# Two products instead of three in every split fp32r projection of a two-block transformer kernel

## What is computed

```
mix = sigmoid(gate_a) * (y_a @ w_o_mla) + sigmoid(gate_b) * (y_b @ w_o_gla)
h = h + mix @ w_out
h = h + peer_ffn(rmsnorm(h, norm_ffn), peer_w_q, peer_keys, peer_u, peer_v)
```

## Time and profile before

| | us |
|---|---|
| median of three runs (lowest, highest) | 2176.15 (2173.21, 2176.32) |
| profiled execution, its span | 2175.9 |
| PE busy | 2115.4 (97%) |
| PE weight loads | 1661.6 (76%) |
| VectorE busy | 1304.1 (60%) |
| GpSimd busy | 1033.5 (47%) |
| ScalarE busy | 922.6 (42%) |
| a weight group's load, issue to landing (median) | 4.8 |

### The profile page before, as it was taken

How to read it: one execution, slowest core, us unless ns; L and a number is a source line. 1 busy time by engine, 2 the same in 40 slices (tenths; PEclk the granted TensorE clock), 3 DMA queues, 4 the chain that set the end, 5 groups by cost and what they waited for, 6 DMA issues and landing times.

```text
span 2175.9 us, 27394 instructions
## 1 busy us (share of the span) xinstructions
PE 2115.4 (97%) x10296; PEld 1661.6 (76%) x10296; DVE 1304.1 (60%) x2244; ACT 922.6 (42%) x1528; POOL 1033.5 (47%) x892
## 2 busy tenths in 40 slices
PE   8999999999999999999999998999999899999999
PEld 6877767557887776887878877777778788888887
DVE  6456257352235774215898957888881666666664
ACT  4223343572234234111334447777773434343432
POOL 6655546212324122877859887999996100000000
PEclk9999999999999999999999999999999999999999
DMA  5222312201111111233216664777788988888884
GB/s 201 100 78 78 116 61 90 90 30 49 59 40 59 59 55 43 97 122 110 78 59 199 205 206 141 272 289 246 272 291 294 333 300 286 289 284 300 288 287 149
DMA packets 98291, 359.32 MB, mean 165 GB/s; under 512 B 8480, under 2 KB 41504, under 8 KB 73328
## 3 DMA queue, kind: packets, MB, share of 16 engines
q1 hardware_dynamic: 98160, 357.56, 47.3%
HBM read 286.09 MB, written 71.30 MB: 164 GB/s over the span
## 4 chain that ended last, share of the span: by engine, by line
PE 67%; POOL 13%; DVE 11%; issue 6%; ACT 2%; DMA 1%; POOLq 0%; SPq 0%; ACTq 0%; DVEq 0%
PE ps L1438 11%; PE ps L1439 11%; PE ps L802 10%; PE ps L803 9%; PE ps L804 9%; POOL area L2643 6%; POOL wring_parts L2621 6%; PE ps L791 2%; PE ps L1249 2%; DVE area L2413 2%; PE ps L1386 1%; PE ps L1387 1%; DVE area L2410 1%; PE ps L884 1%; PE ps L1225 1%
## 5 line engine op out<-in xcount | busy, mean ns | idle before, releaser
L2577 POOL CAST wring_parts<-wring 128x512 fp32r<-128x512 f32 x236 | 170.5, 764 | 546.0 <-PE ps L804 429.3
L1386 PE MATMUL ps<-sqbuf_parts,wring_parts 128*128 128x512 f32 x1024 | 412.6, 403 | 5.5 <-POOL wring_parts L2621 5.5
L1387 PE MATMUL ps<-normed_x_parts,wring_parts 128*128 128x512 f32 x1024 | 404.4, 395 | 0.0
L2621 POOL TENSOR_TENSOR wring_parts<-wring_parts,wring 128x512 fp32r<-128x512 f32 x256 | 331.0, 1323 | 76.0 <-ACT wring_parts L1856 73.0
L2581 POOL TENSOR_TENSOR wring_parts<-wring,wring_parts 128x512 fp32r<-128x512 f32 x244 | 351.2, 1470 | 6.6 <-ACT wring_parts L1852 1.5
L1386 PEld LDWEIGHTS ps<-sqbuf_parts,wring_parts 128*128 128x128 f32 x1024 | 194.0, 189 | 50.6 <-POOL wring_parts L2621 4.9
L1387 PEld LDWEIGHTS ps<-normed_x_parts,wring_parts 128*128 128x128 f32 x1024 | 193.9, 189 | 41.8
L802 PE MATMUL ps<-resid_parts,wring_parts 128*128 128x512 f32 (+1 forms) x528 | 201.2, 381 | 6.1 <-DVE normed_x_parts L2010 3.3
L803 PE MATMUL ps<-normed_x_parts,wring_parts 128*128 128x512 f32 (+1 forms) x528 | 197.0, 373 | 0.0
L804 PE MATMUL ps<-resid_parts,wring_parts 128*128 128x512 f32 (+1 forms) x528 | 196.2, 372 | 0.0
L1474 ACT ACTIVATE area<-ps 128x1024 f32<-128x1024 f32 (+6 forms) x89 | 61.7, 696 | 275.2 <-PE ps L804 183.5
(11 more groups left out here) (269 smaller groups left out, 4431.4 us busy)
## 6 DMA issues: line engine op xcount, KB each, us to landing
wring<-in_weights_dram SPq DMA_DIRECT2D x65, 1024.0 KB, 4.8
wring<-in_uT_dram SPq DMA_DIRECT2D x128, 512.0 KB, 4.4
area<-in_vT_dram SPq DMA_DIRECT2D x44, 1024.0 KB, 7.2
hidden_table<-area SPq DMA_DIRECT2D x32, 1024.0 KB, 6.7
gate_table<-area SPq DMA_DIRECT2D x32, 1024.0 KB, 8.4
area<-gate_table SPq DMA_DIRECT2D x32, 1024.0 KB, 9.1
wring<-in_vT_dram SPq DMA_DIRECT2D x20, 1024.0 KB, 6.7
rt<-hidden_table SPq DMA_DIRECT2D x32, 512.0 KB, 4.6
```

Of the source, the lines that this page charges most:

```text
L1386: pe.matmul(out, first[:, d], h_first[:, k, :], start=(k == 0), stop=False)
L1387: mm = pe.matmul(out, rest[:, d], h_rest[:, k, :], start=False, stop=(k == KD - 1))
L2577: ins = nc.gpsimd.tensor_copy(up[:, d, :], W(name)[:, d, :])
L2621: ins = nc.gpsimd.tensor_tensor(rest[:, a:a + PIECE], first[:, a:a + PIECE], u_raw[t % len(USLOT)][:, a:a + PIECE], ALU.subtract)
```

## The change

Every split product of an activation a and a weight w becomes two fp32r products. With S = 128 and GAIN = 127/128: w_first = rounded GAIN x w, w_rest = w_first - w; a_first = rounded a / S, a_rest = 127 x a_first - a. Then w_first x a_first + w_rest x a_rest is a x w / S, up to terms of the order of the product of two rounding errors. Where nothing else takes the factor up, the result is multiplied by S as it leaves PSUM; for the projections from the normed x, the three gains `pre`, `mix` and `ffn` are multiplied by 128 once at the start, so a needs no more.

- `three` becomes `two`: the matmul of L804 is gone at every use, the other two stay.
- GpSimd's cast (L2577) becomes a `tensor_scalar` multiplication by GAIN, written as fp32r. Its subtraction has its operands turned.
- ACT's copies that round get `scale=1/S` (activations) or `scale=GAIN` (the four weight groups it rounds).
- DVE's subtractions (L1984, L2010, L2061) become `scalar_tensor_tensor` of the same tiles; two of its operations that read PSUM (L2369, L2379) too.
- DVE gets three `tensor_scalar` of 128 x 8 at the start; ACT's squares and copies out of `wo` and `pg` get a scale.

```diff
@@ -796,12 +796,11 @@
                 return W_parts(name)
-            def three(out, a_parts, b_parts, first, last):
-
-                (a_up, a_low), (b_up, b_low) = a_parts, b_parts
-                pe.matmul(out, a_up, b_up, start=first, stop=False)
-                pe.matmul(out, a_up, b_low, start=False, stop=False)
-                return pe.matmul(out, a_low, b_up, start=False, stop=last)
+            def two(out, a_parts, b_parts, first, last):
+
+                (a_first, a_rest), (b_first, b_rest) = a_parts, b_parts
+                pe.matmul(out, a_first, b_first, start=first, stop=False)
+                return pe.matmul(out, a_rest, b_rest, start=False, stop=last)
@@ -822,7 +821,7 @@
                             c = (m - tiles[0]) * 512 + at + (MF.start if width == TM else 0)
-                            mm = three(out[:, c:c + n], (up[:, k, d], low[:, k, d]),
+                            mm = two(out[:, c:c + n], (up[:, k, d], low[:, k, d]),
@@ -1493,33 +1492,33 @@
                 act.activation(r, r, ACT.Exp, scale=-0.5).then_inc(rooted, 1)
-            def square_two(name, m, src, width=T):
+            def square_two(name, m, src, width=T, scale=1.0):
                 dst = sqbuf[:, 0:KD * width].rearrange("p (k t) -> p k t", k=KD)[:, 2 * m:2 * m + 2, :]
-                act.activation(dst, src, ACT.Square).then_inc(squares, 1)
+                act.activation(dst, src, ACT.Square, scale=scale).then_inc(squares, 1)
                 act.wait_ge(gained, 4 * turn + m + 1)
-                act.activation(parts[0][:, 2 * m:2 * m + 2, :], src[:, 2 * m:2 * m + 2, :], ACT.Copy
-                               ).then_inc(gained_up, 1)
+                act.activation(parts[0][:, 2 * m:2 * m + 2, :], src[:, 2 * m:2 * m + 2, :], ACT.Copy,
+                               scale=1.0 / SCALE).then_inc(gained_up, 1)
                 k = slice(2 * m, 2 * m + 2)
-                act.activation(W_parts("q0")[0][:, k, :], W("q0")[:, k, :], ACT.Copy
+                act.activation(W_parts("q0")[0][:, k, :], W("q0")[:, k, :], ACT.Copy, scale=GAIN
             act.wait_ge(w_in[1], 16)
-            act.activation(W_parts("k0")[0], W("k0"), ACT.Copy).then_inc(part_rounded, 1)
+            act.activation(W_parts("k0")[0], W("k0"), ACT.Copy, scale=GAIN).then_inc(part_rounded, 1)
@@ -1531,7 +1530,8 @@
                         act.wait_ge(normed, NORM[name] + 1)
-                    act.activation(h_upper[:, k, 0:width], normed_x[:, k, 0:width], ACT.Copy).then_inc(h_rounded_k, 1)
+                    act.activation(h_upper[:, k, 0:width], normed_x[:, k, 0:width], ACT.Copy, scale=1.0 / SCALE
+                                   ).then_inc(h_rounded_k, 1)
@@ -1562,7 +1562,8 @@
                 act.wait_ge(pair_made, n + 1)
-                act.activation(parts[0][:, k:k + 2, :], src[:, k:k + 2, :], ACT.Copy).then_inc(pair_rounded, 1)
+                act.activation(parts[0][:, k:k + 2, :], src[:, k:k + 2, :], ACT.Copy, scale=1.0 / SCALE
+                               ).then_inc(pair_rounded, 1)
@@ -1611,8 +1612,8 @@
                 when_filled(act, ("wo", m))
-                square_two("post", m, pair(("wo", m)))
-                copy_out(("wo", m), mixedT[:, 2 * m:2 * m + 2, :], pair(("wo", m)))
+                square_two("post", m, pair(("wo", m)), scale=float(SCALE))
+                copy_out(("wo", m), mixedT[:, 2 * m:2 * m + 2, :], pair(("wo", m)), scale=float(SCALE))
@@ -1622,7 +1623,7 @@
             for m in range(4):
-                copy_out(("pg", m), sgT[:, 2 * m:2 * m + 2, :], pair(("pg", m)), ACT.Sigmoid)
+                copy_out(("pg", m), sgT[:, 2 * m:2 * m + 2, :], pair(("pg", m)), ACT.Sigmoid, float(SCALE))
@@ -1849,7 +1850,7 @@
                     act.wait_ge(w_in[WN[name] % NW], 16 * (WN[name] // NW + 1))
-                    act.activation(W_parts(name)[0], W(name), ACT.Copy).then_inc(query_up, 1)
+                    act.activation(W_parts(name)[0], W(name), ACT.Copy, scale=GAIN).then_inc(query_up, 1)
@@ -1875,7 +1876,7 @@
                     act.wait_ge(hid_stored[g % 2], 16 * (g // 2))
-                act.activation(hid_out[g % 2][:, j, :], ps[:, j, :], ACT.Gelu, scale=float(SCALE)).then_inc(gelu_done, 1)
+                act.activation(hid_out[g % 2][:, j, :], ps[:, j, :], ACT.Gelu).then_inc(gelu_done, 1)
@@ -1969,6 +1970,10 @@
                               vec[:, VEC["lam"][0] + 2:VEC["lam"][0] + 4], ALU.mult).then_inc(lam_ready, 1)
+            for name in ("pre", "mix", "ffn"):
+                at, n = VEC[name]
+                ins = dve.tensor_scalar(vec[:, at:at + n], vec[:, at:at + n], float(SCALE), None, ALU.mult)
+            link(ins)
@@ -1981,8 +1986,8 @@
                 x = slice(2 * m, 2 * m + 2)
-                dve.tensor_tensor(parts[1][:, x, :], src[:, x, :], parts[0][:, x, :], ALU.subtract
-                                  ).then_inc(gained_low, 1)
+                dve.scalar_tensor_tensor(parts[1][:, x, :], parts[0][:, x, :], float(SCALE - 1), src[:, x, :],
+                                         ALU.mult, ALU.subtract).then_inc(gained_low, 1)
@@ -2007,8 +2012,8 @@
                     dve.wait_ge(h_rounded_k, KD * turn + k + 1)
-                    dve.tensor_tensor(h_lower[:, k, 0:width], normed_x[:, k, 0:width], h_upper[:, k, 0:width],
-                                      ALU.subtract).then_inc(h_ready, 1)
+                    dve.scalar_tensor_tensor(h_lower[:, k, 0:width], h_upper[:, k, 0:width], float(SCALE - 1),
+                                             normed_x[:, k, 0:width], ALU.mult, ALU.subtract).then_inc(h_ready, 1)
@@ -2058,8 +2063,8 @@
                 dve.wait_ge(pair_rounded, n + 1)
-                dve.tensor_tensor(parts[1][:, k:k + 2, :], src[:, k:k + 2, :], parts[0][:, k:k + 2, :],
-                                  ALU.subtract).then_inc(pair_split, 1)
+                dve.scalar_tensor_tensor(parts[1][:, k:k + 2, :], parts[0][:, k:k + 2, :], float(SCALE - 1),
+                                         src[:, k:k + 2, :], ALU.mult, ALU.subtract).then_inc(pair_split, 1)
@@ -2366,7 +2371,8 @@
                     dve.wait_ge(pair_made, 12 + m)
-                empties(dve.tensor_tensor(mix_tmp, gate_s[:, m % 2, :, :], pair(("ob", m)), ALU.mult), ("ob", m))
+                empties(dve.scalar_tensor_tensor(mix_tmp, pair(("ob", m)), float(SCALE), gate_s[:, m % 2, :, :],
+                                                 ALU.mult, ALU.mult), ("ob", m))
@@ -2376,7 +2382,7 @@
                 x = resid[:, 2 * m:2 * m + 2, 0:T]
-                empties(dve.tensor_tensor(x, x, pair(("w2", m)), ALU.add), ("w2", m))
+                empties(dve.scalar_tensor_tensor(x, pair(("w2", m)), float(SCALE), x, ALU.mult, ALU.add), ("w2", m))
@@ -2574,11 +2580,11 @@
                     for d in parts:
-                        ins = nc.gpsimd.tensor_copy(up[:, d, :], W(name)[:, d, :])
+                        ins = nc.gpsimd.tensor_scalar(up[:, d, :], W(name)[:, d, :], GAIN, None, ALU.mult)
                 for d in parts:
-                    ins = nc.gpsimd.tensor_tensor(low[:, d, :], W(name)[:, d, :], up[:, d, :], ALU.subtract)
+                    ins = nc.gpsimd.tensor_tensor(low[:, d, :], up[:, d, :], W(name)[:, d, :], ALU.subtract)
@@ -2594,7 +2600,7 @@
                         pool.wait_ge(w_in[WN[name]], 16)
-                    ins = nc.gpsimd.tensor_tensor(low[:, k, :], W(name)[:, k, :], up[:, k, :], ALU.subtract)
+                    ins = nc.gpsimd.tensor_tensor(low[:, k, :], up[:, k, :], W(name)[:, k, :], ALU.subtract)
```

More of the change, by code:

```diff
@@ L838, in project_parts @@
                             pe.wait_ge(pair_split, 4 * turn + n // 2 + 1)
-                        mm = three(pair(key)[:, m, :], (up[:, k, d], low[:, k, d]),
+                        mm = two(pair(key)[:, m, :], (up[:, k, d], low[:, k, d]),
                                    (parts[0][:, k, :], parts[1][:, k, :]), n == 0, n == KD - 1)
@@ L850, in tokens_h @@
                     for k in range(KD):
-                        mm = three(flat(key)[0:n, a * 256:a * 256 + 256], h_parts(k, t * P, n),
+                        mm = two(flat(key)[0:n, a * 256:a * 256 + 256], h_parts(k, t * P, n),
                                    (up[:, k, :], low[:, k, :]), k == 0, k == KD - 1)
@@ L925, in first_query @@
                         d = slice(a * P, (a + 1) * P)
-                        mm = three(pair(key)[:, a, :], (up[:, k, d], low[:, k, d]),
+                        mm = two(pair(key)[:, a, :], (up[:, k, d], low[:, k, d]),
                                    (FIRST_PARTS[0][:, k, :], FIRST_PARTS[1][:, k, :]), k == 0, k == KD - 1)
@@ L950, in first_value @@
                     for k in range(KD):
-                        mm = three(flat(key)[:, t * 256:t * 256 + 256],
+                        mm = two(flat(key)[:, t * 256:t * 256 + 256],
                                    (FIRST_PARTS[0][:, k, d], FIRST_PARTS[1][:, k, d]), (up[:, k, :], low[:, k, :]),
@@ L1236, in gate_quarter @@
```

(2 more changed lines are left out.)

## The result

The changed kernel takes 2102.01 us (median of 4 runs, 2100.2 to 2104.5) against 2176.24 us before (4 runs, 2173.21 to 2176.71): a ratio of 0.9655, 95% interval 0.9639 to 0.9672. It is 74 us faster where 166 were forecast, and 2102 lies above the stated range of 1975 to 2075. The profiled execution has a span of 2098.4 us. The removed products are gone and the steps of those that stay are the old ones (231 ns before, 230 ns after, in the output projection); what came back of their 240 us is less than a third.

The account below looks back on a forecast made before the run. TensorE bounds the kernel (67% of the chain), GpSimd where weight groups run dense. Of 240 us removed, stage terms kept 172.8; less 7 for clock and multiplications, 166: 2175.9 to 2010 us, range 1975 to 2075.

Parts of the forecast that it names:

- (a): GpSimd's four casts per weight group become multiplications by a constant, taken at 0.60 us each, between 0.57 and 1.26.
- rival 1: GpSimd's multiplication costs the two-input price, 2.76 us more a group, together 80 us: 2090 us; chance 0.22 for above 2035.
- Rival 3: Slower: a GpSimd multiplication over 1.6 us, some 46 groups binding after 22 us of slack; about 2250 at 2.0; chance 0.03.
- The law behind it: In runs of groups without other TensorE work GpSimd sets the period, 7.4 to 11 us against TensorE's 7.4.
- The prediction's sum by that figure: With the skill's 769 ns for each GpSimd multiplication, some 18 us more than forecast: 2025 us.
- Stages in which GpSimd has slack: Second and third attention's side projections: 31 of 35 us and 13.1 of 15 us kept.
- The first two terms: From the start to 226.9 us, first projections and first attention: 8.6 of 15 us and 45 of 45 kept.
- the 4 that were charged to the clock: Some four more stretches of TensorE at half clock after idling (wo, ckv0, w20, pq2): 4 us lost.
- the marks of the prediction: Dense run from gg0's start: gg3's parts 27.6, ob0's 46.4, w20's 104.5, w21's products end 121.7, pq1's end 159 us.
- the 3.7 us that were to be kept there: After 1053.2 us, 3.7 of 22 us kept, where GpSimd waited 15.17 us at 1134.64 for ACT behind pq7's products.

Follow-up runs that it names:

- e1_cast: The changed kernel with GpSimd's multiplication by the constant replaced by the cast of the kernel before: 2032.47 us, ratio 0.9322.
- e4_one_product: The changed kernel with the second product left out as well, one product for each tile: 2078.35 us, ratio 0.9530.

## Why the prediction was wrong

Time kept up to each place, worked out from the starts of GpSimd's work in the traces of before, of e1_cast and after, beside the prediction's terms (whose borders lie within some us of these, except the third, 395.6 for 424.2, which has no projections between):

```
up to the start of        before    e1_cast    after   predicted   kept e1   kept after
wo1                        226.9      173.6    199.5       53.6      53.3       27.4
pg1                        278.8      221.5    252.6        9.3       4.0       -1.2
gq0                        424.2      359.9    389.4       14.1       7.0        8.6
ta1                        676.1      579.1    611.3       31.0      32.7       30.0
gg1                        812.6      702.5    736.8       13.1      13.1       11.0
pq3                       1054.4      906.3    977.4       48.0      38.0        1.2
first top-k (VectorE)     1056.2      913.0    977.4                 -4.9        1.8
end of the span           2175.9     2032.7   2098.4        3.7       0.0       -1.3
sum                                                       172.8     143.2       77.5
```

**The step that failed** is (a) of "What is added": "One input is what it shares with the cast, so I take 0.60". It measured 1.46 us undisturbed and 1.63 in the mean (the cast before: 0.57 and 0.76). Worse, the bound "Above: the two-input subtraction, 1.26 us" was no bound: the one-input multiplication lies above it, so the range, which stopped short of rival 1's 2090, was built on a wrong upper end. Rival 1 (0.22) was the right mechanism, and its sum of 80 us came near the 66 by which the traces of e1_cast and after differ, but in part by luck. Between these two traces the losses are, with rival 1's in brackets: 5.7 us up to v1's parts (5), 20.2 in the first attention (10), 5.2 in wo (5), -1.6 from pg1 to gq0 (7), 2.7 up to ta1 (3), 2.1 up to gg1 (none), 37 up to pq3 of which 7 come back before the first top-k (41), 1.3 behind that (8). And these come from a price of 1.46; the same arithmetic at 1.46 would have given some 100 (80 x 3.56/2.76). The reason is seen in the dense run: a group lost 2.4 us (12.0 for 9.5 in the mean), not the 3.56 that the free prices differ by, because with the cast GpSimd waits and collides too. Rival 3's arithmetic has the same fault, a full price lost in each of 46 groups: for 1.46 us it gives (0.86 x 4 x 46) - 22 = 136 us, 2146 in all, where 2102 was measured.

**The law behind it held.** "The period is GpSimd's" is what the rows after, e1_cast and e4_one_product show at 10.9, 8.3 and 11.8 us. The Trainium skill's GPSIMD Engine Reference, section 3.1, which the prediction set beside its sum, has 769 ns as the best case for 512 elements; this multiplication took 1460 and the measurement decides. The prediction's sum by that figure, 2025 us, was 77 us short. The same section names a floor of two-input operations by a shared read port; from that alone one would expect the one-input form to be the cheaper, and here the two-input multiplication with one column took 1.01 us.

**Stages in which GpSimd has slack** came out as worked: 31 predicted and 30.0 to 32.7 for the side projections of the second attention, 13.1 and 11.0 to 13.1 for the third. The first two terms at the cast's price, 8.6 and 45, measured 8.7 (to v1's parts) and 44.6. That the scalar_tensor_tensor, the scales and the 8-column multiplications cost next to nothing fits these stages; no run tried them alone.

**The other 25 us** are what e1_cast kept less than forecast: 5 us in wo, 7 from the per-layer gates to the latents, 10 in the dense run, 9 after it, against 2 more in the second attention and the 4 that were charged to the clock. In the dense run GpSimd's group took 10.1 to 10.3 us for gg3, tb0 and ob0 where I had 9.4. Counted from gg0's first product, the marks of the prediction came late by 1 us (gg3's parts), 3 (ob0's), 4 (w20's), 8 (the end of w21's products, behind VectorE's last MIX pair) and 7 (pq1's end, 166 for 159).

The 9 us after it are two things. Ahead of the first top-k TensorE waited for VectorE, whose norm and splits run without a gap from 892.5 to 911.7 us; the first top-k stands at 913 where I had 887. From the first top-k to the end all three kernels take the same, 1119.7, 1119.7 and 1121.0 us, so the 3.7 us that were to be kept there failed: GpSimd's wait for ACT, 15.17 us at 1134.64 before, stayed. Rows of e1_cast:

```profile
906.50 3.75 PE L1376 MATMUL ps<-keys_sb,area 128*128 128x128 f32 x16 [4.38 <-DVE area L2396]
988.69 10.00 POOL L2627 TENSOR_TENSOR wring_parts<-wring_parts,wring 128x512 fp32r<-128x512 f32 x8 [14.33 <-ACT wring_parts L1857]
```

The single wait of 11.7 us of e1_cast ends at 974.5, beside the top-k. What would shorten these places was not tried.

**Clock.** The prediction charged 4 us. After, the granted clock is 0.90 in the dense run against 0.99 to 1.00 before, much more time at the lower level than four stretches, yet nothing shows a cost of its own where GpSimd sets the period: at 0.78 in e4_one_product the group is still GpSimd's. The Trainium skill, TensorE: Matmul & The Clock Gate, Part 1, says that idle gaps throttle TensorE; the trace agrees (0.90). That the 70 us come from it is refuted by e1_cast, where the cast alone brought them back and the clock rose to 0.96 with nothing done to it. Of the other 25 us the clock may hold a part: a mean of 0.96 between the two levels over 203.8 us makes 16 us at the lower one, which could cost at most 8 us, by my estimate from that row. This was not separated.

**Collisions.** These are the same as before. VectorE's subtraction, whose free time is 1.23 us, takes up to 2.32 us before and 2.33 after, in the median 1.63 in both (shortest, median and longest in ns):

```profile
L2061 DVE TENSOR_TENSOR area_parts<-area,area_parts x12: 1210/1627/2320, 217.3 to 986.5; 128x1024 fp32r<-128x1024 f32 x12
L2066 DVE SCALAR_TENSOR_TENSOR area_parts<-area_parts,area x12: 1212/1628/2326, 188.3 to 902.9; 128x1024 fp32r<-128x1024 f32 x12
```

One of them, after:

```profile
843.34 2.18 DVE L2066 SCALAR_TENSOR_TENSOR area_parts<-area_parts,area 128x1024 fp32r<-128x1024 f32 x1 [8.21 <-ACT area_parts L1565]
```

That is 0.95 us over its free 1.23, at a time when GpSimd's subtraction of 839.48 to 844.44 was ending; GpSimd's four multiplications from 844.41 on then took 6.83 for 5.86. The Trainium skill, SBUF — State Buffer, "Who interferes with whom", says that a two-input VectorE instruction and a GpSimd instruction that reads SBUF exclude each other; the trace agrees (0.95 us late here for the one, 0.97 for the other).

## What to carry to other kernels

When a change shortens the bound engine, work out the period of the engine that feeds it first, and price each new operation on that engine by a row of that very operation; where no row has it, neither its count of inputs nor the dearest neighbour is a bound, and the range must reach well past both. When the feeder then binds, spread its work: here one of two steps given to ACT, in halves and ahead of ACT's other work, turned 74 us of gain into 148. Price a group by its mean in the run as well as by its free rows: the free difference was 3.56 us a group, the time lost 2.4. And compare the stages at common marks: the total hides that three of the stages were forecast within 2 us at the old price.

## What the runs showed of the hardware that I had not expected

- GpSimd's `tensor_scalar` multiplication, fp32 to fp32r, takes 1.46 us for 128x512 (1.29 + 0.17 fixed); the cast 0.57, the two-input subtraction 1.25, a two-input multiplication with one broadcast column 1.01. One input fewer was dearer.
- 4 bytes of shift in SBUF of the tensor that holds stationary operands of the last stage lengthened their products from 227 to 233 ns, those with the stationary operand elsewhere not at all, and the kernel by 14 us.
